# Last attention of a two-block transformer kernel: the scaling of the probabilities and the copy of the numerators move from VectorE to ScalarE, and the fold of the two probability tiles moves to the end of VectorE's slot

## What is computed

```python
# 16 query heads of 64 channels, 4 key/value heads, blocks of 128 queries against 256 keys
logits = einsum('btkgd,bskd->bkgts', qb, kb) + alibi        # window mask: -inf outside
m = maximum(max(logits, -1), sink)
p = exp(logits - m[..., None])
denom = sum(p, -1) + exp(sink - m)
o = einsum('bkgts,bskd->btkgd', p, vb) / denom
y = out * silu(z);  return y @ w_out
```

## Time and profile before

| | us |
|---|---|
| median of 3 runs | 2566.18 (2565.63 to 2566.23) |
| the profiled execution's own time | 2566.36 |
| its span | 2564.6 |
| TensorE matmuls busy | 2497.5 (97%) |
| VectorE busy | 1398.5 (55%) |
| ScalarE busy | 1019.0 (40%) |
| GpSimd busy | 1130.0 (44%) |

### The profile page before, as it was taken

The page is one execution under the profiler, slowest core; times in us unless marked ns, Lnnn a source line. Parts: engine busy times, 40 slices in busy tenths (PEclk is TensorE's granted clock), DMA queues, the critical chain, the costliest instruction groups (busy, mean ns, idle before and its releaser), DMA issues.

```text
span 2564.6 us, 41617 instructions
## 1 busy us (share of the span) xinstructions
PE 2497.5 (97%) x15824; PEld 2015.9 (79%) x15824; DVE 1398.5 (55%) x2664; ACT 1019.0 (40%) x1992; POOL 1130.0 (44%) x1390
## 2 busy tenths in 40 slices
PE   7999999999999999999999999999999999999999
PEld 6887777777777777777788878788888888777777
DVE  3002253345866657576632677766666007588843
ACT  4125646556433333242113453555554115344421
POOL 3332222223433243231457545677776554545452
PEclk9999999999999999999999999999999999999999
DMA  4241211211201111011432332333334115101132
GB/s 141 84 131 46 62 55 58 72 56 42 66 23 53 35 34 51 26 59 63 165 127 73 105 103 98 108 99 101 107 106 172 42 56 154 45 26 30 30 114 84
DMA packets 234438, 198.94 MB, mean 78 GB/s; under 512 B 7296, under 2 KB 202240, under 8 KB 233728
## 3 DMA queue, kind: packets, MB, share of 16 engines
q1 hardware_dynamic: 188800, 120.60, 15.6%
q10 hardware_dynamic: 45440, 75.68, 8.3%
HBM read 150.64 MB, written 45.61 MB: 77 GB/s over the span
## 4 chain that ended last, share of the span: by engine, by line
PE 79%; DVE 13%; ACT 5%; issue 2%; POOL 1%; DMA 0%; ACTq 0%; DVEq 0%; SPq 0%; POOLq 0%
PE gemm L808 13%; PE gemm L810 13%; PE gemm L809 13%; PE gemm L1269 5%; PE gemm L1271 5%; PE gemm L1270 5%; PE scores L880 2%; PE weighted L908 1%; PE probs_t L893 1%; DVE neg_logits L2318 1%; PE weighted L1496 1%; PE scores L1347 1%; PE probs_t L1140 1%; DVE prob L2331 1%; DVE prob L2330 1%
## 5 line engine op out<-in xcount | busy, mean ns | idle before, releaser
L758 POOL CAST w_hi<-w_raw 128x512 fp32r<-128x512 f32 x264 | 188.3, 713 | 1182.6 <-PE gemm L810 1039.6
L760 POOL TENSOR_TENSOR w_lo<-w_raw,w_hi 128x256 fp32r<-128x256 f32 x528 | 441.9, 837 | 41.7
L808 PE MATMUL gemm<-h_hi,w_hi 128*128 128x512 f32 x1072 | 449.0, 419 | 1.2 <-DVE h_lo L1964 1.2
L810 PE MATMUL gemm<-h_hi,w_lo 128*128 128x512 f32 x1072 | 420.2, 392 | 0.0
L809 PE MATMUL gemm<-h_lo,w_hi 128*128 128x512 f32 x1072 | 418.9, 391 | 0.0
L1617 DVE CUSTOM_DVE_ANT_0 neg_logits<-scores,bias_tile 128x128 f32<-128x128 f32 (+1 forms) x192 | 67.7, 352 | 339.6 <-PE scores L880 334.4
L808 PEld LDWEIGHTS gemm<-h_hi,w_hi 128*128 128x128 f32 x1072 | 202.1, 189 | 48.1 <-issue 14.2
L810 PEld LDWEIGHTS gemm<-h_hi,w_lo 128*128 128x128 f32 x1072 | 201.2, 188 | 44.2
L809 PEld LDWEIGHTS gemm<-h_lo,w_hi 128*128 128x128 f32 x1072 | 202.4, 189 | 32.7 <-issue 1.7
L808 PE MATMUL gemm<-xn_hi,w_hi 128*128 128x512 f32 x288 | 117.7, 409 | 1.9 <-DVE xn_lo L2235 1.7
L3152 ACT ACTIVATE prob<-neg_logits,stats 128x256 f32<-128x256 f32 (+1 forms) x128 | 63.5, 496 | 135.2 <-DVE stats L2318 132.1
(11 more groups left out here) (639 smaller groups left out, 6126.5 us busy)
## 6 DMA issues: line engine op xcount, KB each, us to landing
w_raw<-in_w_in SPq DMA_DIRECT2D x73, 512.0 KB, 3.9
w_raw<-in_a_w_in SPq DMA_DIRECT2D x28, 512.0 KB, 4.0
w_raw_b<-in_a_w_in SPq DMA_DIRECT2D x20, 512.0 KB, 4.7
gates_scratch<-o_f ACTq DMA_DIRECT2D x32, 256.0 KB, 2.0
merge_gates<-gates_scratch ACTq DMA_DIRECT2D x4, 2048.0 KB, 10.2
mlp_v_scratch<-v_piece ACTq DMA_DIRECT2D x32, 256.0 KB, 2.0
mlp_v<-mlp_v_scratch ACTq DMA_DIRECT2D x16, 512.0 KB, 4.1
w_raw<-in_a_w_out SPq DMA_DIRECT2D x16, 512.0 KB, 4.1
```

The source lines that it names most:

```text
L758: Q(pool.tensor_copy(weight_part(u, 0, ks), raw[:, s, ks, :]))
L760: Q(pool.tensor_tensor(weight_part(u, 1, ks), raw[:, s, ks, :], weight_part(u, 0, ks).bitcast(F32), ALU.subtract), E("w_split") if ks.stop ...
L808: pe.matmul(dst, w_high, hi(k, h), start=first, stop=False)
L810: m = pe.matmul(dst, w_low, hi(k, h), start=False, stop=last)
```

## The change

VectorE's slot loses the scaling (L2331) and the copy of the numerators (L2348). What is left of the normalisation, now `folded2`, is done for pass c, at the end of slot c + 3, instead of for pass c-1 in the middle of the slot. ScalarE begins its slot with four scaled copies of pass c-1 and the numerators' copy of pass c-3. The gating waits for ScalarE's copy. All semaphores have their counts adapted to the new order.

```diff
-            def normalised2(c):
+            def folded2(c):
                 t = c % 4
                 dve.wait_ge(E("exp_done"), len(quads) + c + 1)
                 den, es = den2[:, c % 2, 0:4], den2[:, c % 2, 4:8]
                 V(v.tensor_tensor(den, den, es, ALU.add))
                 V(v.reciprocal(den, den))
                 with_prev = slice(1, 4, 2) if t == 0 else slice(0, 4)
                 own, prev = pr2[:, c % 2, :, P:256], pr2[:, c % 2, :, 0:P]
-                V(v.tensor_tensor(own[:, with_prev], own[:, with_prev], prev[:, with_prev], ALU.add))
-                V(v.tensor_tensor(own, own, den.unsqueeze(2).to_broadcast([P, 4, P]), ALU.mult), E("pn_done"))
+                V(v.tensor_tensor(own[:, with_prev], own[:, with_prev], prev[:, with_prev], ALU.add), E("w_rows"))
...
-            def gated2(c):
-                i, t = c // 4, c % 4
-                dve.wait_ge(E("pv_full"), len(quads) + c + 1)
-                cs = slice(256 * t, 256 * t + 256)
-                V(v.tensor_copy(ys[:, i, cs], PV[:, 0:256]), E("pv_free"))
-
             def gate2(i):
+                dve.wait_ge(E("pv_free"), len(quads) + 4 * i + 4)
                 V(v.scalar_tensor_tensor(ys[:, i, :], ys[:, i, :], 0.5, zs2[:, i % 2, :], ALU.mult, ALU.mult), E("gated"))
...
                 if 0 <= c < 4 * QP:
                     biased2(c)
-                if 0 <= c - 1 < 4 * QP:
-                    normalised2(c - 1)
...
-                if 0 <= c - 3 < 4 * QP:
-                    gated2(c - 3)
...
+                if 0 <= c < 4 * QP:
+                    folded2(c)
...
+            def normalised2(c):
+
+                act.wait_ge(E("w_rows"), PAIRS + c + 1)
+                for x in range(4):
+                    own = pr2[:, c % 2, x, P:256]
+                    A(a.activation(own, own, ACT.Copy, scale=den2[:, c % 2, x:x + 1]), E("pn_done") if x == 3 else None)
+
+            def gated2(c):
+                i, t = c // 4, c % 4
+                act.wait_ge(E("pv_full"), len(quads) + c + 1)
+                A(a.activation(ys[:, i, 256 * t:256 * t + 256], PV[:, 0:256], ACT.Copy), (E("pv_free"), len(quads) + c + 1))
...
             for s in range(S_SLOTS + 1):
                 c = s - 3
+                if 0 <= c - 1 < 4 * QP:
+                    normalised2(c - 1)
+                if 0 <= c - 3 < 4 * QP:
+                    gated2(c - 3)
                 if 0 <= c < 4 * QP:
                     exps2(c)
```

More of the change, by code:

```diff
@@ L2341, in parted2 @@
                 V(v.tensor_tensor(pts2[:, :, P:256], both, causal.unsqueeze(1).to_broadcast([P, 4, P]), ALU.mult))
-                V(v.tensor_tensor(pts2[:, with_prev, 0:P], both[:, with_prev], later[:].unsqueeze(1).to_broadcast([P, n_prev, P]), ALU.mult), E("pt_done"))
-            def gated2(c):
-                i, t = c // 4, c % 4
-                dve.wait_ge(E("pv_full"), len(quads) + c + 1)
-                cs = slice(256 * t, 256 * t + 256)
-                V(v.tensor_copy(ys[:, i, cs], PV[:, 0:256]), E("pv_free"))
+                V(v.tensor_tensor(pts2[:, with_prev, 0:P], both[:, with_prev], later[:].unsqueeze(1).to_broadcast([P, n_prev, P]), ALU.mult), (E("pt_done"), len(quads) + c + 1))
             def gate2(i):
+                dve.wait_ge(E("pv_free"), len(quads) + 4 * i + 4)
                 V(v.scalar_tensor_tensor(ys[:, i, :], ys[:, i, :], 0.5, zs2[:, i % 2, :], ALU.mult, ALU.mult), E("gated"))
```

## The result

| | before | changed |
|---|---|---|
| median (runs) | 2566.18 us (5) | 2576.22 us (5; 2573.51 to 2578.43) |
| ratio, 95% interval | | 1.004, 1.0028 to 1.0052 |
| the profiled execution: own time, span | 2566.36, 2564.6 | 2576.22, 2574.1 |

The change makes the kernel 10.0 us slower. The forecast was 2572.0 us, 5.8 slower than before, in a range up to 2578. The direction is right, the size is short by 4 us.

A forecast was written before the change was run, and what follows sets the result against it. The prediction took a ring of waits through VectorE and ScalarE, 8.0 us a pass, as the bound. Ring +8.5 us less 2.6 of slack at the end gave +5.9, forecast 2572.0 us, range 2565 to 2578.

The forecast's parts named there:

- Rival 3: TensorE's waits for VectorE just go: 14.35 us off, 2551.8 us; chance 0.04.
- VectorE's new wait: Before L2326, for ScalarE's exponentials (L3155): 32 times and over 50 us in total.
- the mean turn: First L2318 of one pass to the next: 8.0 us; forecast wrong if under 7.8 or over 8.2.
- the ring: Parting, logits, exponentials and fold in sequence through VectorE and ScalarE: 247.9 us over 31 turns, 8.5 longer than before.
- logits, exponentials, hand-over: Pieces of the ring on VectorE and ScalarE: 64.5, 96.5 and 3.1 us over 31 turns.
- partings: VectorE, L2341 to first L2318: 1.33 us, narrow 1.07; 30 of them, 37.8 us in the ring.
- The copies: ScalarE's four scaled copies a slot: 0.40 us each, 1.7 us for four, outside the ring.
- cases 4 and 5: Longer ring from GpSimd meetings or overflowing VectorE work, chance 0.14; ScalarE's copies entering the ring, chance 0.04; both 2578 us.
- The first case: Ring at the measured means: +5.9 us, with 1.6 us for 0.05 a turn either way; chance 0.65.
- The end: Last pass's logits to TensorE's last transposes: 8.6 us instead of 11.18, giving back 2.6 us.
- The unsure term: VectorE's fold beside GpSimd: 1.30 us priced, 1.07 without such company, which makes 7.1 us of the ring.
- Case 2: Ring without GpSimd's company at the fold: 239.8 us for the turns, 2563.8 us in all; chance 0.13.

The follow-up runs named there:

- run 3: Changed kernel with VectorE's biased logits of pass c before the parting of pass c-2: 2548.42 us, ratio 0.9931.
- run 6: Changed kernel with one more tiny VectorE instruction (128x4 copy onto itself) between reciprocal and fold: 2582.32 us, ratio 1.0068.
- run 5: Changed kernel with two more 128x128 copies on ScalarE ahead of the four scaled ones in every slot: 2575.99 us, ratio 1.0045.
- run 2: Changed kernel with the fold back in its old place (pass c-1, behind the logits of pass c): 2598.21 us, ratio 1.0127.
- run 8: The changed kernel as it stands, measured once more: 2574.78 us, ratio 1.0042.
- run 1: Changed kernel with the parting's last instruction signalling as before the change, without the explicit count: 2572.22 us, ratio 1.0023.
- runs 1 and 4: The second of these is the changed kernel with the edits of run 1 and run 3 together: 2548.15 us, ratio 0.9930.

## Why the prediction came out as it did

**The mechanism was right.** Rival 3, that the waits just go, was to fail for want of work under the exponentials; it did. VectorE's new wait was put at over 50 us and measured 65.2, the mean turn at 8.0 us (8.10 measured), and TensorE's idle time did not fall (20.98 us). Breaking the ring (run 3), a dose inside it (run 6) and one outside (run 5) all gave the ring's answer, and run 2 gave that of the other ring which was foretold for it. Three signs were less exact: VectorE's busy time fell by 38.0 us in the stretch where about 41 was expected, the turns are not even (7.27 to 8.95 us after the first), and the named waits of TensorE are 12.3 + 5.3 = 17.6 us where over 20 were expected.

**The sum of the ring, piece by piece.** Both profiles of the changed kernel and that of run 1, timed from start to start in VectorE's timeline:

| 31 turns, us | forecast | changed | run 8 | run 1 |
|---|---|---|---|---|
| logits, exponentials, hand-over | 164.1 | 164.5 | 164.3 | 164.0 |
| folds | 40.3 | 39.3 | 38.6 | 40.2 |
| bias tiles | 5.7 | 5.9 | 5.9 | 5.9 |
| partings | 37.8 | 41.4 | 41.4 | 37.9 |
| together | 247.9 | 251.14 | 250.24 | 248.05 |

**The terms that held.** Logits, exponentials and hand-over together were put at 5.42 us, narrow 4.93; from the first L2318 to L2326 they take 5.42 to 5.44 in every wide pass, and 4.94 or 4.95 in the narrow ones. So VectorE's other work was hidden in all of them. The copies take 0.403 us against 0.40, the numerators' copy 0.385 against 0.5.

**The term that was mis-sized is the parting.** It was timed in the trace of before at 1.33 and 1.07 us and carried over. It measures 1.45 and 1.19, since the change gave its last instruction's signal an explicit count (a line that the excerpt of the diff above leaves out; run 1 shows it), and with it a real wait. I had read that line as bookkeeping. In 30 partings this is 3.6 us. Run 1, in which that term is as I priced it, has its median at 2572.2 us, where the forecast was 2572.0. That the two agree so closely is in part luck: the folds alone differ by up to 1.6 us between these profiles.

**The range held by luck.** It reached up to 2578 for cases 4 and 5, and their causes did not come about: the folds were cheaper than priced, no other work of VectorE lengthened the wait for the exponentials, and the copies took 0.403 us. The first case with its 1.6 us either way ends at 2573.6 and does not hold 2576.22.

**The end**: 8.88 us instead of 8.6. The step that was wrong is that a tanh or a high part before ScalarE's copies would still fit. In the last pass both stand before them:

```profile
2463.50 1.14 DVE L2330 TENSOR_TENSOR prob<-prob 128x512 f32<-128x512 f32 x1
...
2463.02 1.06 ACT L3164 ACTIVATE swa_y_hi<-swa_y 128x1024 fp32r<-128x1024 f32 x1
2464.11 0.63 ACT L3182 ACTIVATE z_silu<-scaled_product 128x512 f32<-128x512 f32 x1
2464.78 1.70 ACT L3155 ACTIVATE prob<-prob,stats 128x128 f32<-128x128 f32 x4
```

The last fold met GpSimd too and took 1.6 us, but that is not the reason. In run 1 it took 1.14, ending 0.6 us before the copies could start behind the tanh, and the last transposes came after 8.86 us all the same. The 12.65 us behind them were to stay, and were 14.10 in the profile. The clock explains this, below.

**The unsure term, GpSimd's company at the fold, stayed.** The Trainium skill (SBUF — State Buffer, "SBUF: two separate sides") has ScalarE free of that port's lock: the trace agrees, with 128 copies of 0.401 to 0.408 us each. But taking the scaling off VectorE did not free the fold: L2330 went from 0.779 to 0.764 us only. Case 2 is out. The prediction also took too much to leave the port: the gate's product and the gating have both inputs in SBUF as well, so that the scaling was 27.7 of 76.3 us of such work, a third and not half, and these two became longer (0.842 to 0.904 and 1.277 to 1.352 us).

## What to carry to other kernels

When a step is moved on one engine's queue, write down the ring that it closes: every piece from the wait back to the same wait, over both engines, with start-to-start times. Where that sum exceeds the bound engine's slot, the ring sets the pace, whatever the busy shares say; then look for a step that need not stand in the ring and put it under the wait (here two calls exchanged, 28 us). Read each changed signal of a diff as an instruction: the wait on one's own completion cost 0.12 us a time here, and only where it stood in the ring (runs 1 and 4).

## What was not expected of the hardware

**An own wait that doesn't bind lets VectorE overlap two instructions.** L2318 starts 0.60 to 0.61 us behind a 0.69 us instruction without it, and 0.72 to 0.73 with it. The Trainium skill (VectorE: DVE Perf Modes, "The DRAIN you can't avoid") gives equal times for a chain of copies with and without semaphores and says that the semaphore costs nothing extra there; the same section has an instruction that is not held start earlier. For this pair the runs show a difference of 0.12 us, and the measurement decides.

**After equal pauses TensorE's clock fell in some executions and not in others.** In the changed kernel's first profile TensorE waits 1.85 us before the last transposes, and then (columns as in the earlier trace rows; the granted clock is the third number from the end):

```profile
2465.00:2470.00 5.00, 3.46 (x24) 2.77 (x25) 4.39 (x7) 2.78 (x7) 4.53 (x7) 0.80 0.09 12
2470.00:2475.00 5.00, 5.00 (x24) 3.76 (x25) 3.17 (x3) 1.09 (x2) 2.96 (x3) 0.86 0.25 96
```

```profile
2468.82 0.63 PE L809 MATMUL gemm<-xn_lo,w_hi 128*128 128x512 f32 x1
2469.24 0.63 PE L810 MATMUL gemm<-xn_hi,w_lo 128*128 128x512 f32 x1
...
2473.03 0.40 PE L810 MATMUL gemm<-xn_hi,w_lo 128*128 128x512 f32 x1
2473.26 0.39 PE L808 MATMUL gemm<-xn_hi,w_hi 128*128 128x512 f32 x1
```

Matmuls start 0.42 to 0.43 us apart at the lower level of 1.2 GHz, and 0.23 at 2.4. The stretch from transposes to output product is 1.6 us longer than in run 8 (14.10 against 12.51). There TensorE stood before the same transposes for 1.84 us, and the granted clock remained 1.00:

```profile
2465.00:2470.00 5.00, 4.21 (x31) 3.45 (x32) 4.51 (x6) 2.11 (x5) 4.53 (x7) 1.00 0.20 45
```

Three other runs leave the order of the queues as in the changed kernel. Run 5 has a pause of 1.84 us at this place, a granted clock below 1.00 behind it and 14.07 us to the output product; run 6 has a pause of 1.83 us and run 1 one of 1.67, both with the clock at 1.00 and 12.53 us. In run 5 a pause of 1.90 us, before the transposes at 2238.80, passed without a fall. So a pause of this length can stand before a fall and need not bring one. What decides it stays open.

The clock also goes with the changed kernel's spread (5 us, against 2 before). Of its ten executions (the first five and run 8), the five with a mean granted clock of 0.996 took 2576.22 to 2578.55 us, and the five with 0.997 took 2573.51 to 2575.35. So the first median, 2576.22, has more of the lower clock in it than that of run 8, 2574.78; the forecast had no term for this.
